# Rotary embedding: the exchange of half-heads by ScalarE's DMAs in place of a TensorE product

## The reference

```
def rope(t, pos):                     # t: one 64-wide query or key
    half = t.shape[-1] // 2
    ang = pos[:, None] * inv[None, :]
    t1, t2 = t[..., :half], t[..., half:]
    return concatenate([t1 * cos(ang) - t2 * sin(ang), t2 * cos(ang) + t1 * sin(ang)], axis=-1)
```

## Time and profile before

| | |
|---|---|
| median of 3 runs | 2001.89 us (2001.58 to 2002.07) |
| the profiled execution | 1995.7 us, its span 1993.9 us |
| TensorE, matmul | 1868.1 us busy, 94% |
| VectorE | 1430.3 us busy, 72% |
| ScalarE | 1190.6 us busy, 60% |
| GpSimd | 140.2 us busy, 7% |
| mean granted TensorE clock | 0.963 |

### The profile page before, as it was taken

One profiled execution on the slowest core, in us unless ns is written; L12 is line 12 of the kernel. 1 busy time (PEld: TensorE's weight loads), 2 busy tenths in 40 slices (PEclk: granted clock), 3 DMA queues, 4 the chain that ended last, 5 costly groups with the idle time before them and its releaser, 6 DMA issues.

```text
span 1993.9 us, 28837 instructions
## 1 busy us (share of the span) xinstructions
PE 1868.1 (94%) x10456; PEld 1590.2 (80%) x10456; DVE 1430.3 (72%) x1525; ACT 1190.6 (60%) x1312; POOL 140.2 (7%) x184
## 2 busy tenths in 40 slices
PE   5999799998689999878999999999999999999997
PEld 5888698777689998877887878878878788787885
DVE  5544365526965556975888878888888788787885
ACT  5553355526454445644677676776676766777774
POOL 0211011112500000700000000000000000000000
PEclk9999999989889999987999999999999999999998
DMA  6311333115335445343998889989889899888991
GB/s 249 144 55 54 139 122 106 47 63 183 117 127 190 163 152 171 108 149 112 349 342 335 344 316 354 356 316 351 341 330 347 327 348 353 324 344 319 357 348 75
DMA packets 67748, 464.88 MB, mean 233 GB/s; under 512 B 7888, under 2 KB 8560, under 8 KB 15696
## 3 DMA queue, kind: packets, MB, share of 16 engines
q1 hardware_dynamic: 66960, 461.15, 61.6%
q0 software_dynamic: 704, 2.63, 0.4%
HBM read 462.71 MB, written 1.05 MB: 233 GB/s over the span
## 4 chain that ended last, share of the span: by engine, by line
PE 85%; DVE 9%; ACT 3%; issue 2%; DMA 0%; ACTq 0%; SPq 0%; DVEq 0%
PE bank L395 24%; PE bank L396 24%; PE bank L397 24%; DVE wlo L386 3%; PE bank L874 2%; PE bank L486 2%; PE bank L882 2%; DVE cacc L1455 2%; DVE csq L1455 1%; ACT whi L381 1%; PE bank L911 1%; PE bank L562 1%; PE bank L559 1%; DVE rstd L1268 1%; PE bank L599 1%
## 5 line engine op out<-in xcount | busy, mean ns | idle before, releaser
L386 DVE TENSOR_TENSOR wlo<-raw,whi 128x2048 fp32r<-128x2048 f32 (+2 forms) x454 | 1011.5, 2233 | 277.0 <-ACT whi L381 276.1
L381 ACT ACTIVATE whi<-raw 128x2048 fp32r<-128x2048 f32 (+2 forms) x454 | 843.9, 1862 | 264.0 <-PE bank L397 262.0
L395 PE MATMUL bank<-whi,hthi 128*128 128x512 f32 x896 | 366.7, 409 | 7.8 <-DVE wlo L386 7.8
L396 PE MATMUL bank<-wlo,hthi 128*128 128x512 f32 x896 | 355.9, 397 | 0.0
L397 PE MATMUL bank<-whi,htlo 128*128 128x512 f32 x896 | 355.8, 397 | 0.0
L395 PE MATMUL bank<-uhi,whi 128*128 128x272 f32 (+2 forms) x1072 | 322.0, 300 | 30.5 <-DVE ulo L1285 20.2
L396 PE MATMUL bank<-ulo,whi 128*128 128x272 f32 (+2 forms) x1072 | 312.8, 292 | 0.0
L397 PE MATMUL bank<-uhi,wlo 128*128 128x272 f32 (+2 forms) x1072 | 312.7, 292 | 0.0
L395 PEld LDWEIGHTS bank<-uhi,whi 128*128 128x128 f32 (+1 forms) x1072 | 209.5, 195 | 35.0 <-issue 22.2
L396 PEld LDWEIGHTS bank<-ulo,whi 128*128 128x128 f32 (+1 forms) x1072 | 209.8, 196 | 0.5
L397 PEld LDWEIGHTS bank<-uhi,wlo 128*128 128x128 f32 (+1 forms) x1072 | 209.0, 195 | 0.0
(11 more groups left out here) (284 smaller groups left out, 2329.7 us busy)
## 6 DMA issues: line engine op xcount, KB each, us to landing
raw<-in_wm SPq DMA_DIRECT2D x338, 1024.0 KB, 4.9
raw<-in_w SPq DMA_DIRECT2D x66, 1024.0 KB, 4.9
raw<-in_w SPq DMA_DIRECT2D x18, 768.0 KB, 4.1
raw<-in_w SPq DMA_DIRECT2D x16, 704.0 KB, 3.9
raw<-in_w SPq DMA_DIRECT2D x14, 512.0 KB, 3.6
raw<-in_w SPq DMA_DIRECT2D x2, 576.0 KB, 4.2
h_in<-in_hT SPq DMA_DIRECT2D x1, 1088.0 KB, 9.5
gmb<-in_gmb POOLq DMA_DIRECT2D x1, 1024.0 KB, 6.9
```

Source lines behind the costliest of these rows:

```text
L381: act.activation(whi[:, n % RING, 0:c], raw[:, n % RAW, 0:c], ACT.Copy).then_inc(hi_ready, 1)
L386: dve.tensor_tensor(wlo[:, n % RING, 0:c], raw[:, n % RAW, 0:c], whi[:, n % RING, 0:c].bitcast(F32), ALU.subtract).then_inc(lo_ready, 1)
L395: pe.matmul(out, s_hi, m_hi, start=start, stop=False, skip_group_check=shared)
L396: pe.matmul(out, s_hi, m_lo, start=False, stop=False, skip_group_check=shared)
```

## The change

`turn` no longer has the product with `rot`, and the load of `rot` is gone. Behind the copy of a q or k tile, ScalarE waits for that copy and issues four DMAs of 32 partitions x 272 elements each (34 KB), which write the exchanged tile to a new SBUF buffer `qswap` (2 buffers). On VectorE the two instructions of the rotary embedding leave `turned(s-1)` for a new function `rotated(s-2)`, called behind `turned` in each slot: those of a tile come one slot later than before, and those of a k tile behind the copies of its head's v tile. The sine product reads SBUF in place of PSUM.

```
@@ turn_uses
-        if kind in ("q", "k") and g < DIFF_HEADS:
-            uses["rot", 2 * g + (kind == "k")] = len(uses)
+PARTNERS = 4
-N_PAR, PAR2, CONST2 = 5, 11, 3
+N_PAR, PAR2, CONST2 = 4, 11, 3
@@ build_program
+        qswap = sb("qswap", [P, 2, LEN], scope=first)
-        rot = sb("rot", [P, P], scope=first)
@@ sync
-            for dst, name in ((bforget, "bforget"), (rope, "rope"), (rot, "rot"), (ident, "ident"), (mask, "mask")):
+            for dst, name in ((bforget, "bforget"), (rope, "rope"), (ident, "ident"), (mask, "mask")):
@@ tensor: turn
-                if kind in ("q", "k") and g < DIFF_HEADS:
-                    r = 2 * g + (kind == "k")
-                    if r == 0:
-                        pe.wait_ge(par_landed, 16 * N_PAR)
-                    pe.wait_ge(proj_taken, l * PROJ_T + (i + 1))
-                    turn_free(l, ("rot", r))
-                    pe.matmul(bank[2][:, 0:LEN], rot[:], qraw[:, r % 2, :], start=True, stop=True).then_inc(rot_done, 1)
@@ scalar: take_tile
                     if r >= 2:
-                        act.wait_ge(rot_done, l * ROPED + (r - 1))
+                        act.wait_ge(swap_taken, l * ROPED + (r - 1))
                         act.wait_ge(rc_ready, l * ROPED + (r - 1))
                     act.activation(qraw[:, r % 2, :], src, ACT.Copy).then_inc(proj_taken, 1)
+                    act.wait_ge(proj_taken, l * PROJ_T + (i + 1))
+                    for part in range(PARTNERS):
+                        to, at = slice(32 * part, 32 * part + 32), slice(32 * (part ^ 1), 32 * (part ^ 1) + 32)
+                        act.dma_start(qswap[to, r % 2, :], qraw[at, r % 2, :]).then_inc(swap_landed[r % 2], 16)
@@ vector
-            def turned(l, i):
+            def rotated(l, i):
                 kind, g = TILE_OF.get(i, ("", 0))
                 if kind in ("q", "k") and g < DIFF_HEADS:
                     r = 2 * g + (kind == "k")
                     if r == 0:
                         dve.wait_ge(par_landed, 16 * N_PAR)
-                    dve.wait_ge(rot_done, l * ROPED + (r + 1))
+                    dve.wait_ge(swap_landed[r % 2], 16 * PARTNERS * (l * (ROPED // 2) + (r // 2 + 1)))
                     if r:
                         dve.wait_ge(roped, l * ROPED + r)
-                    dve.tensor_tensor(rsn[:], bank[2][:, 0:LEN], rope[:, 2 * (r % 2) + 1, :], ALU.mult).then_inc(turn_taken, 1)
-                    dve.wait_ge(turn_taken, l * TURNS + (TURN_USES["rot", r] + 1))
+                    dve.tensor_tensor(rsn[:], qswap[:, r % 2, :], rope[:, 2 * (r % 2) + 1, :], ALU.mult).then_inc(swap_taken, 1)
+                    dve.wait_ge(swap_taken, l * ROPED + (r + 1))
                     dve.wait_ge(rc_ready, l * ROPED + (r + 1))
                     if g >= 2:
                         dve.wait_ge(s_done, l * MAPS + 2 * (g - 1))
                     dve.tensor_tensor(qk[:, 2 * (g % 2) + r % 2, :], rc[:, r % 2, :], rsn[:], ALU.add).then_inc(roped, 1)
+            def turned(l, i):
+                kind, g = TILE_OF.get(i, ("", 0))
                 if kind == "v":
@@ vector: the order of the slots
                 for s in range(SLOTS):
                     turned(l, s - 1)
+                    rotated(l, s - 2)
```

## The result

The changed kernel takes 2014.27 us (median of 4, 2010.62 to 2018.82) against 2001.98 us: a ratio of 1.0063, 95% interval 1.0042 to 1.0083, so 8 to 17 us slower. Measured again beside other runs it is 2015.90 us, ratio 1.0073 (1.0049 to 1.0098). The forecast was 2007.2 us, 5.3 us slower, with 2004.5 to 2012 as its own range: right in direction, less than half of the size.

What follows compares the result with a forecast made beforehand. TensorE, with 85% of the chain, was taken as the bound. Late scores, 2.5 us over both layers, plus 2.8 for the clock gave 5.3 us slower, 2007.2 us; whole range 1999.5 to 2014, the forecast's own 2004.5 to 2012.

Steps and rivals of the forecast that it cites:

- What the products give: TensorE: sixteen products with `rot` removed at 0.46 us each, one a layer giving nothing, so 6.4 us at most.
- one product hidden behind the difference: Fourth head: its q product stands right ahead of TensorE's wait for the difference, so removing it gives nothing.
- The price of an issue: ScalarE: each DMA issue costs 0.40 us, bounds 0.33 and 0.49; with the wait, 1.7 us a tile.
- my own working for head 1: Layer 0, first head: ScalarE's issues delay `split_hi`, then VectorE; scores start at 44.7 against 41.85, 2.85 us late.
- Heads 2 and 3 win back 0.8 us each: Second and third head: lateness of the scores falls from 2.85 us to 2.05, then to 1.25.
- The clock: TensorE after head 1's idle time: three microseconds at half clock, 1.5 us of work lost; 2 x 1.4 = 2.8 us.
- VectorE's order: k's rope behind the v copies: scores wait 1.65 us behind the transposes, of which `meet_values` covers 1.50 in heads 2, 3.
- The landing: Exchange into `qswap`: VectorE asks 5.7 us after k's last issue in head 1, 6.0 in head 2; costed at nothing.
- a rival for slow DMAs: Exchange lands late: if a small DMA needs 8 us, scores wait 2.3 us more a head; about 2025 at most; chance 0.05.
- The cheap-issue: Rival: ScalarE's issues cost under 0.1 us, head 1 only 0.45 late; -2.2 us, 1999.7; chance 0.13.
- the faster rivals: Issues under 0.1 us and two of TensorE's slow stretches in the attention part vanish: -5.2 us, 1996.7; chance 0.07.
- ScalarE as the bound: Rival: issues cost 0.8 us or more; head 1 3.2 us later than forecast; about +18 us, 2020; chance 0.09.

Runs made afterwards that it cites:

- Without an exchange: Changed kernel with no DMAs, the sine product reading the tile itself (wrong rotation), no product on TensorE, VectorE in the new order: 2001.35 us, 1.0012.
- issues of 0.44 us: Changed kernel with its four DMAs a tile on ScalarE reading a constant in HBM instead of the tile in SBUF (wrong rotation): 2008.92 us, 1.0031.
- the second run: The changed kernel unaltered, measured again beside the other runs: 2015.90 us, 1.0073.
- one issue a tile: Changed kernel with one 128-partition straight copy a tile by ScalarE instead of four DMAs, so no exchange and a wrong rotation: 2000.68 us, 0.9974.
- neither pair of runs: Rope behind the v copies against rope first: with no exchange DMAs 1.0012 and 0.9998, in the changed kernel 1.0073 and 1.0069.
- SyncE's exchange behind a load: Changed kernel with the same four DMAs a tile issued by SyncE between its weight loads, none by ScalarE: 2009.96 us, 1.0056.
- four issues a head: Changed kernel with one set of four DMAs a head on ScalarE, behind the k copy, moving q and k together: 2008.78 us, 1.0040.
- SyncE's early set: Changed kernel with SyncE issuing four DMAs a head, q and k together, the first set ahead of unit 8's load, rope first: 1998.31 us, 0.9975.

## Why the prediction was off

- **What the products give**: right in sum, in part by luck. Without an exchange the stretch of layer 1 fell from 66.65 to 65.23 us, both at full clock, 1.4 for my 1.1. By heads the changes were +0.67, -0.94, -0.65 and -0.51 us for my +0.45, -0.80, -0.75 and 0. So in the fourth head, where I had one product hidden behind the difference and the other paid back by the rope, half a microsecond came out; that made up for a first head later than forecast.
- **The price of an issue**: the term that was mis-sized. I took 0.40 us from SyncE's rows, with 0.49 as the upper bound; it was 0.61, and 0.82 on average in the first set (3.29 for four). SyncE's rows were loads from HBM; the same engine paid 0.59 for this exchange. "Their sizes run from under 1 KB to 1 MB, so size hardly sets it" held, but size was not what differed. A tile costs ScalarE 2.5 us, not 1.7. In my own working for head 1 two tiles more by 0.85 and the long first set by 0.85 turn 2.85 us late into 5.4; measured 5.33. In layer 1, without so long an issue, it was 4.85.
- **Heads 2 and 3 win back 0.8 us each**: wrong, from the same term. From scores to scores layer 0 took 18.6 and 17.4 us for before's 17.04 and 17.30. A part of the 18.6 is the clock; the rest is that VectorE's path, behind eight issues, stayed the longer one (waits of 0.97 and 0.91 us). With issues of 0.44 us these waits were 0.2 us. The schedule lost 3.3 us a layer and not 1.25.
- **The clock**: the mechanism was expected, its size was low by half or more. I took one half-clock stretch of 3 us a layer, 1.4 us; the two layers lost 3.6 and 8.6, in the second run 5.3 and 3.6. Behind head 1's idle time the half clock lasted 6.8 us in each layer, and layer 1 had it in two more places. Idle times of 3.0 us or more ahead of head 1's transposes or scores had half clock at the scores in every run that had one. Shorter ones did not decide it: 1.5 us was followed by half clock with one issue a tile and not without an exchange, and the wait of 2.3 us for the difference was followed by it in layer 0 of the kernel before and not in layer 1. No run held the clock fixed, so that idle time brings it on is argued and not shown.
- **VectorE's order**: nearly hidden as said in heads 2 and 3. Set first it saves about 2 us a layer at full clock where ScalarE is on time and 1 to 2 where it is late, and in neither pair of runs does the time show it.
- **The landing**: hidden in the changed kernel as forecast, VectorE never waits for it. But it decides as soon as a set is late: 5.27 us of wait with SyncE's exchange behind a load. That was put down as a rival for slow DMAs; a queue's order makes it just as well.
- **The cheap-issue and the faster rivals** needed issues under 0.1 us and fell. ScalarE as the bound was put at 0.8 us an issue; at 0.61 it was already true in part, and the time that lay between the two cases was where I had left little room. The 1.5 us in that rival's own sum has no source either. The Trainium skill (DMA: Bandwidth & Descriptors, Anatomy of one DMA) gives some 50 ns for a sequencer's dispatch and about 2 us of fixed cost, but for DMAs that GpSimd issues. ScalarE and SyncE issue these, so the 50 ns are no price for them: no issue in the rows above took less than 0.31 us. The landings here took 1.8 us at the least and 2.7 at the median.

## What to carry to other kernels

A DMA that a compute engine issues is an instruction in that engine's order: count the issues, price them by a row of the same form (source, partitions), and ask what stands behind them. Here 64 issues of 0.6 us cost more than the 16 products of 0.46 us that they replaced, while the same exchange in 32 issues on SyncE, with only weight loads behind them and the rope first on VectorE, gave a small gain. Where an idle queue issues them, put them ahead of anything that waits for the work which they are to overtake.

## What was not expected of the hardware

- An issue from SBUF to SBUF of 32 (or 16) partitions takes 0.61 us on ScalarE and 0.59 on SyncE, of 128 partitions 0.47, of 32 partitions from HBM 0.44, and SyncE's 1 MB loads 0.33. Bytes make no difference (34 and 68 KB both 0.61).
- Single issues take two to three times the median, at places that change from run to run: up to 1.36, 1.83 and 1.61 us in the changed kernel, with four issues a head, and with SyncE's early set.
- Executions of one program spread by 24 us (before: 1991.0 to 2015.0) on one core. The mean granted clock goes with it: 0.965 in the fastest, 0.952 in the slowest.
